# Rwkv's removal keys ahead of the decays' exponentials, one exponential to a value unit, and value gates between the removal products

## The reference, cut to what matters

```python
shifted = jnp.pad(h, ((0, 0), (1, 0), (0, 0)))[:, :-1]
xm = h[:, :, None, :] + (shifted - h)[:, :, None, :] * mix      # six mixes
rkv = jnp.einsum('bsjd,jde->bsje', xm[:, :, :3], w_rkv)
r, k, v = rkv[:, :, 0], rkv[:, :, 1], rkv[:, :, 2]
logw = -softplus(-(w0 + jnp.tanh(xw @ w1) @ w2)) - 0.5
decay = jnp.exp(-jnp.exp(logw))
a = sigmoid(a0 + (xa @ a1) @ a2)
g = sigmoid(xg @ g1) @ g2
if v_res is not None:                                             # second Rwkv layer only
    v = v + (v_first - v) * sigmoid(v0 + (xv @ v1) @ v2)
kk = heads(k * k_k)
kk = kk * lax.rsqrt(jnp.maximum(jnp.sum(kk * kk, axis=-1, keepdims=True), 1e-24))
# step: state = state * w - (state @ kk) * (kk * a) + v * k;  y = state @ r
```

## Time and profile before

| | |
|---|---|
| time, median of 3 runs | 2342.1 us (2340.4 to 2342.15) |
| the profiled execution | 2340.44 us, its span 2338.4 us |
| PE busy | 2235.1 us, 96% of the span |
| DVE busy | 1552.6 us, 66% |
| ACT busy | 1210.3 us, 52% |
| DMA queue of the loads | 322.66 MB, 40.9% of 16 engines |
| mean granted clock of PE | 0.987 |

### The profile page before, as it was taken

The page is one execution under the profiler, slowest core; times in us unless marked ns, Lnnn a source line. Parts: engine busy times, 40 slices in busy tenths (PEclk is TensorE's granted clock), DMA queues, the critical chain, the costliest instruction groups (busy, mean ns, idle before and its releaser), DMA issues. The chain is left out here.

```text
span 2338.4 us, 55662 instructions
## 1 busy us (share of the span) xinstructions
PE 2235.1 (96%) x23008; PEld 2146.5 (92%) x23008; DVE 1552.6 (66%) x2401; ACT 1210.3 (52%) x2061; POOL 35.9 (2%) x51
## 2 busy tenths in 40 slices
PE   6899899999999999999988998999999999999998
PEld 6799899999999988899977998999998999888998
DVE  7754465566665688665587644655776777876776
ACT  5643454455544456644466434544677444776443
POOL 0000000000000010000000000000100000100000
PEclk9899999999999999999998999999999999999999
DMA  5310255543455433355433102554433555434553
GB/s 201 126 47 4 71 191 188 173 144 118 154 196 188 153 118 119 126 201 191 156 99 127 47 4 85 187 188 168 148 116 129 180 197 171 136 118 142 191 184 112
DMA packets 88435, 327.14 MB, mean 140 GB/s; under 512 B 9808, under 2 KB 9936, under 8 KB 87632
## 3 DMA queue, kind: packets, MB, share of 16 engines
q1 hardware_dynamic: 87984, 322.66, 40.9%
q0 software_dynamic: 288, 2.10, 0.3%
HBM read 323.67 MB, written 1.05 MB: 139 GB/s over the span
## 5 line engine op out<-in xcount | busy, mean ns | idle before, releaser
L2050 PE MATMUL bank<-h_split,w_split 128*128 128x256 f32 x3176 | 913.4, 288 | 22.4 <-DVE h_split L2269 8.6
L2051 PE MATMUL bank<-h_split,w_split 128*128 128x256 f32 x3176 | 898.7, 283 | 0.0
L2052 PE MATMUL bank<-h_split,w_split 128*128 128x256 f32 x3176 | 898.4, 283 | 0.0
L2238 DVE TENSOR_TENSOR w_split<-ring_a,w_split 128x1024 fp32r<-128x1024 f32 x474 | 568.1, 1224 | 192.2 <-ACT w_split L2135 190.9
L2050 PEld LDWEIGHTS bank<-h_split,w_split 128*128 128x128 f32 x3176 | 604.0, 190 | 35.0 <-DVE h_split L2269 11.3
L2051 PEld LDWEIGHTS bank<-h_split,w_split 128*128 128x128 f32 x3176 | 599.2, 189 | 1.4
L2052 PEld LDWEIGHTS bank<-h_split,w_split 128*128 128x128 f32 x3176 | 598.1, 188 | 0.0
L2135 ACT ACTIVATE w_split<-ring_a 128x1024 fp32r<-128x1024 f32 x474 | 483.5, 1049 | 47.9 <-PE bank L594 25.8
L2072 PE MATMUL bank<-act_split,d_split 128*128 128x256 f32 x1008 | 285.4, 283 | 3.8 <-DVE act_last L2330 2.4
L2073 PE MATMUL bank<-act_split,d_split 128*128 128x256 f32 x1008 | 285.2, 283 | 0.0
L2074 PE MATMUL bank<-act_split,d_split 128*128 128x256 f32 x1008 | 285.1, 283 | 0.0
(11 more groups left out here) (282 smaller groups left out, 3235.6 us busy)
## 6 DMA issues: line engine op xcount, KB each, us to landing
ring_a<-wa SPq DMA_DIRECT2D x474, 512.0 KB, 4.0
ring_d<-wd SPq DMA_DIRECT2D x132, 512.0 KB, 4.5
tab_sb<-tab SPq DMA_DIRECT2D x1, 2384.0 KB, 13.3
hT<-na POOLq DMA_DIRECT2D x2, 1024.0 KB, 5.2
xT<-x SPq DMA_DIRECT2D x1, 1024.0 KB, 4.9
out<-xT SPq DMA_DIRECT2D x1, 1024.0 KB, 3.9
vec_sb<-vec SPq DMA_DIRECT2D x1, 288.0 KB, 4.9
tab_sb<-tab SPq DMA_DIRECT2D x1, 65.0 KB, 4.6
```

What stands on the lines that cost most here:

```text
L2050: mm(dst, w[:, 0, ks], x[:, 0, k, :], start=(k == 0), stop=False)
L2051: mm(dst, w[:, 0, ks], x[:, 1, k, :], start=False, stop=False)
L2052: last = mm(dst, w[:, 1, ks], x[:, 0, k, :], start=False, stop=(k == KT - 1))
L2238: v.tensor_tensor(w_split[:, u % 4, 1, :], ring_a[:, u % 4, :], w_split[:, u % 4, 0, :].bitcast(f32), ALU.subtract).then_inc(s["w_lo"], 1)
```

## The change

Three edits, all in the Rwkv layers, and no instruction is added or removed.

1. DVE: the removal keys stand behind the low splits of units 16 and 17 (were: 18 and 19); the second four scans behind that of unit 18 (were: ahead of 15). Group 5's mixes begin behind the low splits of units 19 and 20, and the low split of unit 21 stands behind all of them.
2. ACT: `decays` is cut into `falling` and `rising`; one exponential follows the evacuation of each of value units 14 to 17. High parts of group 5 stand behind the second falling and the second rising one, and split 21 behind the last of them.
3. DVE, second layer: the first four value gates stand in twos ahead of each of the two products with `a`, where they stood behind both and the low split of unit 24; a `settle` (a wait for DVE's own last steps) is added ahead of them.

```diff
--- before.py
+++ after.py
@@ -724,11 +724,12 @@
                 A(cum[:, n, :], B[b][:, cols], ACT.Sigmoid, bias=V(f"w0_{j}", n))
                 A(qkv[:, n, :], B[b + 1][:, cols], ACT.Sigmoid, bias=V(f"a0_{j}", n)).then_inc(s["lora2_ready"], 1)
 
-            def decays(h):
+            def falling(h):
 
                 act.wait_ge(s["cum_done"], 8 * r + 4 * h + 4)
-                ch = slice(16 * h, 16 * h + 16)
-                A(dec[:, ch, 1:CH + 1], half_rows(cum, h), ACT.Exp, scale=-KAPPA)
+                A(dec[:, 16 * h:16 * h + 16, 1:CH + 1], half_rows(cum, h), ACT.Exp, scale=-KAPPA)
+
+            def rising(h):
                 A(half_rows(cum, h), half_rows(cum, h), ACT.Exp, scale=KAPPA).then_inc(s["dec_ready"], 1)
             evac(9, 8, 16)
             split(13)
@@ -744,14 +745,16 @@
                 split(13 + m)
                 if m < 4:
                     xm_hi(4, m)
-                if m in (4, 7):
-                    xm_hi(5, (m - 4) // 3)
+                evac(10 + m, 8 + m, 16 + m)
                 if m in (4, 6):
-                    decays(m // 2 - 2)
-                evac(10 + m, 8 + m, 16 + m)
-            split(21)
+                    falling(m // 2 - 2)
+                if m in (5, 7):
+                    rising(m // 2 - 2)
+                if m >= 6:
+                    xm_hi(5, m - 6)
             for p in range(2, 4):
                 xm_hi(5, p)
+            split(21)
             split(22)
             act.wait_ge(s["a_used"], u + 20)
             step.did(A(work[:, 5, :], B[1][:, 0:S], ACT.Sigmoid))
@@ -1006,24 +1009,29 @@
             for m in range(8):
                 if m < 4:
                     mixed(4, m)
-                if m in (1, 2):
-                    for n in range(4 * m - 4, 4 * m):
+                if m == 1:
+                    for n in range(4):
                         running(n)
                 low(13 + m)
                 if m < 4:
                     mixed_low(4, m)
-                if m in (5, 6):
-                    for n in range(4 * m - 20, 4 * m - 16):
+                if m in (3, 4):
+                    for n in range(4 * m - 12, 4 * m - 8):
                         removal_key(n)
-                if m in (4, 7):
-                    mixed(5, (m - 4) // 3)
-                    mixed_low(5, (m - 4) // 3)
-
-            low(21)
+                if m == 5:
+                    for n in range(4, 8):
+                        running(n)
+                if m >= 6:
+                    mixed(5, m - 6)
+                    if m == 7:
+                        mixed_low(5, 0)
+
+            mixed_low(5, 1)
             mixed(5, 2)
             mixed(5, 3)
             mixed_low(5, 2)
             mixed_low(5, 3)
+            low(21)
             low(22)
             dve.wait_ge(s["gate_hi"], r + 1)
             v.tensor_tensor(work_r[:, 5, :], work[:, 5, :], work_r[:, 4, :].bitcast(f32), ALU.subtract)
@@ -1049,9 +1057,13 @@
                 for h in range(2):
                     step.did(v.tensor_tensor(both_halves(v_first, h), both_halves(v_first, h), values(h), ALU.subtract))
                 dve.wait_ge(s["v1_mm"], 1)
+                step.settle()
             else:
                 dve.wait_ge(s["a_used"], u + 18)
             for h in range(2):
+                if j:
+                    value_gate(2 * h)
+                    value_gate(2 * h + 1)
                 ins = v.tensor_tensor(half_rows(oT, h), rows(0, h), rows(24, h), ALU.mult)
                 if h == 0:
                     step.did(ins)
@@ -1059,9 +1071,6 @@
             low(24)
             step.settle()
             dve.wait_ge(s["a_read"], r + 1)
-            if j:
-                for n in range(4):
-                    value_gate(n)
             for h in range(2):
                 dve.wait_ge(s["dec_ready"], 2 * r + h + 1)
                 last = v.tensor_tensor(half_rows(oT, h), half_rows(oT, h), half_rows(cum, h), ALU.mult)
```

## The result

The changed kernel takes 2330.17 us (median of 5, 2327.73 to 2330.51) against 2342.1 before (2340.4 to 2342.38): a ratio of 0.9949, interval 0.9935 to 0.9963, so 12 us or 0.5% faster, with 9 to 15 us inside the interval. Run again later beside the kernel before, it was 8.7 us faster (ratio 0.9966). Its profiled execution has a span of 2328.5 us against 2338.4. The forecast was 2332.8, range 2327 to 2338.8.

A forecast was written before the change was run, and what follows sets the result against it. PE was taken as the busy engine, held up mainly by 7.08 us waits for late removal keys and by clock falls. Gains of 4.2 (layer 1) and 5.1 (layer 2) sum to 9.3 us: median 2342.1 to 2332.8, range 2327 to 2338.8.

The forecast's parts named there:

- The 7.08 us waits: PE's wait for the removal keys after unit 17, once in each Rwkv layer; claimed to go entirely.
- Group 5 at 97.0, and a new PE wait of 4.3 and 1.5 us: Layer 1's x_split group 5 ready at 97.0 instead of 102.6; PE waits for it before unit 20, layers 1 and 2.
- ACT's new wait for the scans: On ACT, before the second falling exponential; delays group 5's high part and split 20 by 1.8 us, claimed to cost nothing.
- Gates at 102.3 and 6.6 us earlier in layer 2: First gate on PE: at 102.3 instead of 106.47 in layer 1, at 1267.2 in layer 2.
- The table load costs 1.3 us: ACT's switch of function table: 1.3 us by the trace, against the skill's 1283 ns plus a 1380 ns drain.
- gain 4.2: Layer 1's term: gates start at 102.3 instead of 106.47 and their own time stays as it is.
- gain 5.1: Layer 2's term: clock falls after two gates, which gives 4.8; 5.1 taken, nearer the middle of 3.2 and 6.9.
- the 1.50 us wait: Layer 2, PE waiting for a gate ACT had not read out; claimed to go with the value gates between removal products.
- caps layer 2 at 6.9: At full clock, DVE's low split of unit 25 limits layer 2's gain to at most 6.9 us.
- Full clock through the gates of both layers: Rival 1: the clock holds through the gates; gain 13 to 15.8 us, 2326.3 at best; chance 0.13.
- The second rival: Gates run wholly at half clock, because a PE wait stands right ahead; gain 3.5 us, 2338.6; chance 0.12.
- Half clock beyond unit 23: Rival 4, slower: half clock stays through the seven units after unit 23; 2370 us; chance 0.04.

The follow-up runs named there:

- the filled kernel: Changed kernel with matmuls that nobody reads put into PE's two waits of each Rwkv layer: 2330.98 us, ratio 0.9962 to the kernel before.
- the exponentials in pairs: Changed kernel with falling and rising exponentials together again, behind the evacuations of units 14 and 16: 2328.0 us, ratio 0.9958 to the kernel before.
- the split moved: Changed kernel with layer 2's low split of unit 25 right behind the value gates on DVE: 2328.49 us, ratio 0.9946 to the kernel before.

## Why the prediction was right, point by point

- **The 7.08 us waits go.** Right. It rested on two conditions, keys and low split 18, both met before PE's end of unit 17. The run with the keys alone shows that the second was the harder one: without the rest of the reorder PE keeps 5.7 us, for low split 18.
- **Group 5 at 97.0, and a new PE wait of 4.3 and 1.5 us.** Measured 96.69 with everything 0.39 earlier, so 97.08, and waits of 4.47 and 1.60.
- **ACT's new wait for the scans costs nothing.** The wait was 1.61 us; DVE's wait for split 20, which the working had, was 1.65.
- **Gates at 102.3 and 6.6 us earlier in layer 2.** Measured 101.90 + 0.39 = 102.29, a shift of 37.43 - 33.25 = 4.2; and 39.77 - 33.21 = 6.56. In layer 1 the clock fell in the wait for group 5 and ran unit 20 at half level, as taken.
- **The table load costs 1.3 us.** The load at 79.39 follows an evacuation that ends at 79.37, and the exponential starts at 80.69; no drain is seen, so that this trace, too, speaks against adding 1.4 us for it.
- **Layer 1's gates take as long as before (gain 4.2).** The size was off: 33.13 us from the first gate to the transposes against 34.61, because half clock took 6.6 us and not 10.4. Gain 5.66. The second profile of the changed kernel, with 10.4 again, has 34.64.
- **Layer 2's gates fall to half clock after about two gates (gain 5.1).** The mechanism was right: the clock fell at about 1262.3, in the second gate. The size was off the other way. The gates took 13.85 us, where 13.4 was worked out, since half of a gate more ran at half clock (that gate took 1.50 us, the six behind it 1.88 each), and unit 23 ran 22 matmuls at half level, to 1279.24, where the working left it as before. Gain 3.90. The two errors nearly cancel, 9.56 against 9.3, and that is luck: which stretches the clock takes in layer 1 the prediction could not know. The median missed by 2.6 us on the good side (2330.17 against 2332.8), of which 2.0 are spread that the sum does not hold.
- **The value gates between the products take the 1.50 us wait away.** They do at full clock. In the changed kernel the gates ran at half, and undoing the edit cost nothing (70.73 against 70.69). The step counted a wait that the slower gates had removed already; it did no harm, since the clock's ends bounded layer 2 in any case.
- **At full clock the low split of unit 25 caps layer 2 at 6.9.** Seen in the filled kernel and with the exponentials in pairs: a wait of 3.2 us there. In the profile of the pairs, with no half clock behind the first gate, layer 2 gained 74.59 - 67.50 = 7.09 us.
- **Rivals.** Full clock through the gates of both layers (0.13) came up in the profile of the pairs, and layer 1 then gained 8.41 and layer 2 7.09, together 15.5, close to the 15.8 that was its end. In the changed kernel itself it did not come. The second rival, half clock through all gates of both layers (0.12), did not come either; layer 2 alone was near it, with six gates of eight, in all four profiles that have the changed kernel's order up to the gates, the wait of 2.02 us ahead of them, and nothing filled. It named the cause that fits layer 2, the wait right ahead of the gates; in layer 1 no such wait stood there. Half clock beyond unit 23 was seen nowhere in the changed kernel.

## What to carry to other kernels

When a wait names one instruction, list every condition that has to be met at that place and work out when each comes; here the named one alone was worth nothing (1.0006), and the reorder of both queues 9 to 12 us. Where PE stands idle ahead of matmuls of few rows, ask what its clock does there: in layer 2 two waits of 1.6 and 2.0 us went with 17.2 us at half clock behind them, and with these waits filled the gates ran at full clock. And an edit that takes away a wait should be judged in the state in which that wait exists: the third edit was worth 0 us in two kernels and 2.9 us of the profile in a third.

## What was not expected of the hardware

The kernel's spread of some 6 us between executions (2336.0 to 2342.4 for the kernel before, 23 of them side by side) has its likely cause in the granted clock, since the same order of work gets different stretches of it: the four with a mean granted clock of 0.988 took 2336.0 to 2337.6, the four with 0.985 took 2341.1 to 2342.4. The run with the third edit alone leaves layer 1 as it was: its first gate is at 37.45 against 37.43, but its transposes are at 67.81 against 72.04, with no half-clock time behind the first gate against 10.4 us. So 10.4 us at 1.2 GHz cost 4.2 us there. In layer 2 of the changed kernel, however, the stretch repeated in four profiles (17.2, 17.3, 17.3, 17.3, counting the kernels with the third edit undone and the split moved), as closely as the view tells; why it repeats there and not in layer 1 is open.
